# Second-layer outer weight sums formed in DRAM by accumulating transfers during the recurrent stage

## The reference

```
merged = (jax.nn.sigmoid(gate_a) * (att @ p['w_branch_a'])
          + jax.nn.sigmoid(gate_b) * (rwkv_y @ p['w_branch_b']))
x = x + merged @ p['w_out']
hm = _rmsnorm(x, p['norm_mlp'])
x = x + jnp.square(jax.nn.relu(hm @ p['w_mlp_in'])) @ p['w_mlp_out']
```

## Time and profile before

| what | value |
|---|---|
| median of three runs | 2492.46 us |
| the three runs | 2480.7, 2492.46 and 2493.25 us |
| the profiled execution's own time | 2478.53 us |
| span in that profile, first to last instruction | 2476.8 us |
| PE busy over the span | 92% |
| DVE busy | 65% |
| ACT busy | 33% |
| POOL busy | 18% |
| mean granted PE clock, share of full | 0.969 |

### The profile page before, as it was taken

How to read it: one execution, slowest core, us unless ns; L and a number is a source line. 1 busy time by engine, 2 the same in 40 slices (tenths; PEclk the granted TensorE clock), 3 DMA queues, 4 the chain that set the end, 5 groups by cost and what they waited for, 6 DMA issues and landing times. The chain is left out here.

```text
span 2476.8 us, 48938 instructions
## 1 busy us (share of the span) xinstructions
PE 2284.6 (92%) x19275; PEld 1701.0 (69%) x19275; DVE 1603.3 (65%) x3005; ACT 806.6 (33%) x1425; POOL 434.4 (18%) x354
## 2 busy tenths in 40 slices
PE   6999999999899999898899889999999999989986
PEld 4566788765656566665665668787778778878865
DVE  3257888965556565345557556648975775776687
ACT  4235888424334342224455532111121111111101
POOL 0020000000000000001101102025354354344340
PEclk8989999999999999898999999999999999999998
DMA  6441232343232313247877744505226326315402
GB/s 188 121 119 63 64 104 71 122 151 102 57 102 59 97 47 105 76 109 225 284 244 258 235 177 148 170 21 200 81 65 191 102 65 184 109 56 178 124 1 81
DMA packets 270656, 306.78 MB, mean 124 GB/s; under 512 B 56230, under 2 KB 183047, under 8 KB 270300
## 3 DMA queue, kind: packets, MB, share of 16 engines
q1 hardware_dynamic: 195316, 252.78, 32.3%
q10 hardware_dynamic: 75112, 50.87, 7.3%
HBM read 239.78 MB, written 62.23 MB: 122 GB/s over the span
## 5 line engine op out<-in xcount | busy, mean ns | idle before, releaser
L1286 PE MATMUL rwkv_banks<-gate_sides_then_att_T 128*128 128x384 f32 (+1 forms) x768 | 280.4, 498 | 7.8 <-PEq L441 3.7
L1286 PEld LDWEIGHTS rwkv_banks<-gate_sides_then_att_T 128*128 128x128 f32 x768 | 139.4, 197 | 76.5 <-issue 19.4
L3606 DVE TENSOR_TENSOR merged_then_hidden<-merged_then_hidden,ps_mm 128x544 f32<-128x544 f32 x180 | 127.8, 715 | 81.9 <-PE ps_mm L3331 78.1
L3331 PE MATMUL ps_mm<-gate_sides_then_att_T,w_mm 128*128 128x272 f32 x584 | 147.6, 400 | 7.8 <-ACT merged_then_hidden L3399 5.4
L600 PE MATMUL first_banks<-hT,w_pr 128*128 128x384 f32 (+3 forms) x432 | 144.3, 491 | 4.6 <-PEq L188 4.6
L3331 PEld LDWEIGHTS ps_mm<-gate_sides_then_att_T,w_mm 128*128 128x128 f32 x584 | 113.0, 194 | 33.3 <-ACT merged_then_hidden L3399 5.8
L910 DVE TENSOR_SCALAR_CACHE_REDUCE _and_tildes_then_k_pages<-scores,mid 128x384 f32<-128x384 f32 (+4 forms) x150 | 131.5, 876 | 3.1
L600 PEld LDWEIGHTS first_banks<-hT,w_pr 128*128 128x128 f32 (+1 forms) x432 | 81.0, 192 | 62.2 <-issue 21.3
L3413 ACT ACTIVATE merged_then_hidden<-merged_then_hidden 128x1088 f32<-128x1088 f32 x32 | 35.6, 1111 | 260.6 <-DVE merged_then_hidden L3618 260.6
L3331 PE MATMUL ps_mm<-right_blocks,w_mm 128*128 128x272 f32 x408 | 101.8, 394 | 3.3 <-DVE sums_of_right_sides_ L3606 3.3
L2376 POOL MEMSET gate_sides_then_att_T<- 128x136 f32 x1 | 0.2, 212 | 596.3 <-POOLq L1181 596.3
(11 more groups left out here) (619 smaller groups left out, 5227.1 us busy)
## 6 DMA issues: line engine op xcount, KB each, us to landing
v_pages<-in_cache_v SPq DMA_DIRECT2D x128, 256.0 KB, 5.3
gate_sides_then_att_T<-in_w_in ACTq DMA_DIRECT2D x46, 512.0 KB, 4.3
_and_tildes_then_k_pages<-in_cache_k SPq DMA_DIRECT2D x88, 256.0 KB, 3.4
gate_sides_then_att_T<-right_blocks_d SPq DMA_DIRECT2D x82, 272.0 KB, 2.7
right_blocks<-right_blocks_d SPq DMA_DIRECT2D x65, 272.0 KB, 2.7
T_and_gates_then_weights<-in_w_mlp_in SPq DMA_DIRECT2D x16, 1024.0 KB, 5.2
T_and_gates_then_weights<-in_w_mlp_out SPq DMA_DIRECT2D x16, 1024.0 KB, 5.5
w_pr<-in_w_in SPq DMA_DIRECT2D x27, 512.0 KB, 5.2
```

Source lines behind the costliest of these rows:

```text
L1286: ins = MM(B[:, gate_bank(n), 0:w], gw[:, n % 2, k_, :], hc[:, k_, 0:w], start=(k_ == 0), stop=(k_ == KO - 1))
L3331: ins = nc.tensor.matmul(ps[:, bank, 0:272], w, right[:, k, :], start=(k == 0 and step in f.OPENS), stop=(k == 1), skip_group_check=True)
L3606: V.tensor_tensor(to, of, f.pair(ps, q, step), ALU.add).then_inc(f.by_dve, 1)
```

## The change

The outer sums of second layers are no longer made by DVE. A new method, called by POOL's program of the recurrent stage after its memsets, makes them in a DRAM tensor `sums_d` (4 sums x 4 groups x 1 MB), each as a copy and an accumulating transfer, and POOL waits for each transfer before it issues the next. That is 8 transfers a group and 32 in all. The accumulation can only add, so S2, S3 and S4 are formed with the opposite sign of a11 or a12, and the signs of the spreading of results follow (DVE's `spread_results`, same number and size of operations). In the MLP stage SP loads, for each second layer, seven pieces of 1 MB (a11, a12, a22 and the four sums) in place of four. `weight_sums` runs for first layers alone. In second layers S2 lies in the buffer s4 and S4 in the buffer s2 (`left_2`), so that each of the seven is loaded when the quarter that stands at the same place in the layer before has finished.

```diff
+    def add_in_dram(self, pool, w_2, r, which):
+        to = dict(zip(("s1", "s2", "s3", "s4"), self.sums_d[:, r]))
+        w = w_2.rearrange("(r k c) (m e) -> k m r c e", k=2, c=512, m=2)
+        a11, a12, a21, a22 = w[0, 0, r], w[1, 0, r], w[0, 1, r], w[1, 1, r]
+        for name, (u, v) in (("s1", (a21, a22)), ("s3", (a21, a11)), ("s2", (to["s1"], a11)), ("s4", (to["s2"], a12))):
+            if name in which:
+                for of, op in ((u, None), (v, ALU.add)):
+                    if op:
+                        self.nc.gpsimd.dma_start(to[name], of, accum_op=ALU.add).then_inc(self.w_sums, 16)
+                    else:
+                        self.nc.gpsimd.dma_start(to[name], of).then_inc(self.w_sums, 16)
+                    self.sums_made += 16
+                    pool.wait_ge(self.w_sums, self.sums_made)
...
             p.clear_last(pool)
-
+            for r in range(FF // D):
+                p.add_in_dram(pool, a["w_mlp_out"], r, ("s1", "s3", "s2", "s4"))
...
+    held = {**quarter, "s1": s1, "s2": s2, "s4": s4}
+    summed_before = ("s1", "s4", "a21", "s2")
+    left_2 = {**left, "P6": s4, "P3": s2}
...
-        if name in ("P1", "P4", "P2"):
-            n = {"P1": "a11", "P4": "a22", "P2": "a12"}[name]
-            if layer % 2:
-                eng.wait_ge(q_in[n], 16 * layer + 16)
-            else:
-                eng.wait_ge(q_scaled[n], 2 * layer + 4)
+        if layer % 2:
+            n = {"P1": "a11", "P4": "a22", "P2": "a12", "P5": "s1", "P6": "s4", "P7": "a21", "P3": "s2"}[name]
+            eng.wait_ge(q_in[n], 16 * (layer + 1 if n in quarter else (layer + 1) // 2))
+        elif name in ("P1", "P4", "P2"):
+            eng.wait_ge(q_scaled[{"P1": "a11", "P4": "a22", "P2": "a12"}[name]], 2 * layer + 4)
         else:
-            eng.wait_ge(l_summed, 4 * layer + {"P5": 1, "P6": 2, "P7": 3, "P3": 4}[name])
+            eng.wait_ge(l_summed, 2 * layer + {"P5": 1, "P6": 2, "P7": 3, "P3": 4}[name])
...
+                users = [{"a11": "P1", "a12": "P2", "a21": "P7", "s1": "P5", "a22": "P4", **more}
+                         for more in ({"s2": "P6", "s4": "P3"}, {"s4": "P6", "s2": "P3"})]
                 for n in range(2 * R):
-                    for name, user, sums in (("a11", "P1", 3), ("a12", "P2", 4), ("a21", "P7", 3), ("a22", "P4", 1)):
+                    r = n // 2
+                    order = layers[n - 1] if n else UP
+                    user = users[(n + 1) % 2]
+                    for name in sorted(held if n % 2 else quarter, key=lambda name: order.index(user[name])):
...
-                        if n % 2:
+                        if n % 2 and name in summed_before:
+                            src = p.sums_d[summed_before.index(name), r]
+                        elif n % 2:
...
-                for n in range(2 * R):
+                for n in range(0, 2 * R, 2):
```

More of the change, by code:

```diff
@@ L3100, in merge_and_mlp @@
     gate_in = [p.sem(f"mm_gate_in{n}") for n in range(2)]
-    q_in, q_scaled = ({n: p.sem(f"ml_{what}_{n}") for n in quarter} for what in ("in", "scaled"))
+    q_in = {n: p.sem("ml_in_" + n) for n in held}
+    q_scaled = {n: p.sem("ml_scaled_" + n) for n in quarter}
     moved = [p.sem(f"ml_moved{n}") for n in range(f.RING)]
@@ L3224, in inner_sums @@
             def inner_sums(q):
-                base, to = left[names[q]], inner[q % 2]
+                base, to = (left, left_2)[q // 7 % 2][names[q]], inner[q % 2]
                 def free(step):
@@ L3278, in product @@
             def product(q, step):
-                name, base, e = names[q], left[names[q]], inner[q % 2]
+                name, base, e = names[q], (left, left_2)[q // 7 % 2][names[q]], inner[q % 2]
                 r, first_layer = q // 14, q % 14 < 7
@@ L3561, in weight_sums @@
                     if n:
-                        dve.wait_ge(*f.product(nth[n - 1]["P6"], "P4"))
+                        dve.wait_ge(*f.product(nth[n - 1]["P3"], "P4"))
                     else:
                         dve.wait_ge(d.made, 14 * ML)
-                    dve.wait_ge(l_summed, 4 * n + 1)
+                    dve.wait_ge(l_summed, 2 * n + 1)
                     V.tensor_tensor(s2, s1, a11, ALU.subtract).then_inc(l_summed, 1)
@@ L3646, in spread_results @@
                 last = nth[2 * R - 1]
-                for after, step, pairs in (("P1", "P4", ((x11, y1),)), ("P5", "P4", ((x12, y5), (x22, y5))),
-                                           ("P6", "P4", ((y6, y1), (x12, y6))),
-                                           ("P7", "P4", ((y7, y6),)), ("P4", "P3", ((x21, y7), (x22, y7)))):
-                    for n, (to, of) in enumerate(pairs):
+                for after, step, sums in (("P1", "P4", ((x11, x11, y1, ALU.add),)),
+                                          ("P5", "P4", ((x12, x12, y5, ALU.subtract), (x22, x22, y5, ALU.add))),
+                                          ("P6", "P4", ((y6, y6, y1, ALU.subtract), (x12, x12, y6, ALU.subtract))),
+                                          ("P7", "P4", ((y7, y6, y7, ALU.subtract),)),
+                                          ("P4", "P3", ((x21, x21, y7, ALU.add), (x22, x22, y7, ALU.add)))):
+                    for n, (to, u, v, op) in enumerate(sums):
                         for m, rows in enumerate((up, down)):
@@ L3654, in spread_results @@
                                 dve.wait_ge(*f.kept(last[after], step))
-                            ch.done(V.tensor_tensor(to[:, rows, :], to[:, rows, :], of[:, rows, :], ALU.add))
+                            ch.done(V.tensor_tensor(to[:, rows, :], u[:, rows, :], v[:, rows, :], op))
             weave(merge_out(), x_sums(), right_blocks(), weight_sums(), rstds(), gather(), finish(), hidden_sums(),
```

23 lines of the change are left out of this document (12 added, 11 removed).

## The result

The changed kernel takes 2500.26 us in the median against 2489.93 us for the kernel before, measured side by side: ratio 1.0050, 95% interval 1.0033 to 1.0067 (a ratio here and below is not the quotient of the two medians, which is 1.0041 in this case). The forecast was 2467 us, with a range that ended at 2494. The profiled execution has a span of 2498.7 us and took 2500.46 us in all.

What follows compares the result with a forecast made beforehand. PE was taken to bound the MLP and recurrent stages, with small holes. 26.8 us won less 6 and 2 paid gave 18.8, so 2478.5 became 2460 us, plus 7 for the median: 2467 us, range 2450 to 2494.

Steps and rivals of the forecast that it cites:

- The recurrent stage, opening: Recurrent stage's first units: gate weight loads land late beside POOL's transfers and PE waits; 6 us taken, 0 to 7.1.
- The recurrent stage, the rest: Recurrent stage after its opening: DVE's operations may be held by POOL; 2 us taken, bounds 0 and 17.
- The chain of POOL: Recurrent stage: POOL's 32 transfers one after another take 427 us, 170 to 613, ending some 160 us before the stage.
- The overrun: First rival, recurrent stage: transfers over 18.5 us each make all engines wait for POOL; 2574 us at 22 each; chance 0.13.
- The MLP part: MLP second layers: PE's holes beside DVE's outer sums go, 26.8 us won in layers 1, 3, 5 and 7; 12 at least.
- the hidden sums of 2.49 us stay where they were: MLP second layers: DVE's hidden sums remain unchanged, and banks are free in time with little to spare.
- The extra loads at nothing: MLP stage: twelve more 1 MB loads on SP's queue cost nothing; without cover each late block costs up to 5.3 us.
- The recurrent stage pays all along: Second rival: each transfer holds a DVE operation 1.0 us, 17 us reach the path, 2477 us, no change; chance 0.16.
- the 8 in the sum: Recurrent stage's cost in the forecast: 6 us for the opening and 2 us for the rest.
- Holes stay: Third rival, MLP: DVE stays late by hidden sums and spreading, only POOL's wait goes; 2475 us; chance 0.13 with the fourth.
- signs of being wrong: POOL last at the recurrent stage's end; gate loads landing in 7 us or more; idle over 2 us before hidden sums.
- The median: Whole kernel: median after put 7 us above the profiled execution's 2460 us, half way between; 2467 us.

Runs made afterwards that it cites:

- e10: The changed kernel with the recurrent stage's 46 gate weight loads cut to one eighth of their rows: 2483.09 us, ratio 0.9984 to the kernel before.
- e12: The changed kernel with gate weight loads cut to one eighth and the gates' stores issued from SyncE's queue: 2482.05 us, ratio 0.9965 to the kernel before.
- e9: The changed kernel with its 32 transfers spread over the recurrent stage behind its opening, one about every 17 us: 2496.23 us, ratio 1.0040 to the kernel before.
- e8: The changed kernel with transfers moved to the projection stage and two POOL waits for hidden sums per second layer: 2462.84 us, ratio 0.9907 to the kernel before.
- e5: The kernel before, unchanged, run once more for a second trace of its recurrent stage: 2491.27 us, one run.

## Why the prediction was wrong, step by step

**The recurrent stage, opening: right in kind, somewhat short.** I took 6 us (0 to 7.1) for late gate weight loads. At before's 585.9 us, behind the opening, the changed kernel's trace was 9.6 us late, and the five others with its loads and transfers in that place were 6.8 to 10.8; the kernels without transfers were 0.0 to 1.3. The waits are those that I named, and with small loads the lateness was gone (e10, e12).

**The recurrent stage, the rest: the step that failed.** "2 us for the rest of the stage", bounds 0 and 17. By the times it is 25 us less the opening's 7 to 10, so 15 to 18 us, and by the traces more. I had measured slack for the loads ("several us to spare") and stopped there. What I put at next to nothing without a row are two consumers of the same engines that have no slack at all: a store whose issuing instruction stands on the engine that computes, and TensorE's instructions. By experiment the first is worth some 7 us, give or take 6; the second, with the lower clock behind its pauses, is argued from traces at about 10 of idle time and as much again of slower products. The first could have been read before: in the kernel before the store at 695.34 us took 1.85 us, beside two loads of 768 KB, where the median is 0.51. And my bound of 17 came from a mechanism, DVE held by POOL, that does not happen here: VectorE's operations kept their lengths. It was near to the size by chance.

**The chain of POOL: right in kind, too long.** 427 us taken, 277 measured, below the middle of 170 to 613. An adding transfer takes 9 to 10 us where I took 16.0, a copy between sums 5.7 where I took 10.7. A copy takes hardly longer than a load alone, 5.3 us, so reading and writing overlap. The overrun did not come. Nor did the rule of the Trainium skill show that I had weighed (SBUF — State Buffer, section "Who interferes with whom"), by which a fast one-source operation and POOL's descriptor writing lock each other out: VectorE's durations are unchanged, and POOL's issuing instructions took 0.5 to 1.3 us.

That the transfers were quicker is no comfort, though. They put the same bytes into less time, and in e9 twice the time made no difference that could be measured.

**The MLP part: right in kind, 26.8 us taken, 11 to 15 measured by the times and 16.8 in the trace.** By layers: 3.0 forecast and 3.1 in the trace, 7.0 and 2.4, 9.6 and 6.7, 7.2 and 5.5; layer 0 lost 1.0. The holes beside the outer sums went (2.43 us in layer 7 became 0.38). In layer 3 the hole in front of P3 was 2.40 us and not the 4.09 that I had read in layer 7 and taken for all three. What failed is the sentence "the hidden sums of 2.49 us stay where they were": they stayed, and became 4.09 and 3.55 us, since POOL's sums now run at the same time. Three holes of 2.52 us, 7.6 us, are most of the 10 that are missing in the trace; without POOL beside them they are 1.3 us each (e8), so not all of it is POOL's. The earlier trace rows had the sign: the second pair of hidden sums, beside POOL, took 4.10 us there, and I wrote that down as a hole of another kind.

**The extra loads at nothing: right.** The loads of second layers land in 5.2 to 5.6 us in the median, 5.5 before, and first layers stay at 89.84.

**The rivals.** "The recurrent stage pays all along" (0.16) is what happened, by other mechanisms. Its 17 us on top of the 8 in the sum make 25, the size that was measured, and that is luck. "Holes stay" happened in part. Together they give the sign: the sum for the profiled kind of execution was -26.8 + 8, and is -15 + 25. Of the signs of being wrong only the last came, idle times over 2 us beside the hidden sums. POOL was not the last at the end of the stage, and the gate weight loads landed in 5.7 us in the median, not in 7.

**The median.** I added 7 us since the median lay above the profiled execution. A good part of the reason is in the table: that execution had an unusually short recurrent stage, 8.4 us under that of e5, which took 12.7 us longer in all.

## What to carry to other kernels

Idle transfer engines are not free room in a stage of many short steps: ask who needs those engines with no slack, and count the stores that a computing engine issues and TensorE's instruction stream among them. The same 32 MB cost 25 us among some 4200 short products and nothing measurable among 1200 long ones, and neither spreading them nor dropping the adding helped measurably; moving them did. And when a change frees an engine from a wait, look at what it will run beside: the freed engine's work can slow its neighbour's.

## What the runs showed of the hardware that I had not expected

- TensorE's instructions arrive as 16 KB transfers over the shared engines, about one for 250 of them. In this stage that is one each 8 us, and with the transfer engines busy at 0.84 the pauses next to them grow from 10 to 12 us to 19 to 25.
- An instruction that issues a transfer can hold its engine: 7.18 us on ScalarE, with the work behind it in order. With loads of 64 KB in front of it in place of 512 KB the longest was 1.20 us (e10). The Trainium skill (DMA: Bandwidth & Descriptors, section "Queues, rings and completion order") says that each transfer engine goes around the queues that have work, a packet at a time. With that the small transfers should not wait for whole megabytes, and the trace agrees: the median gate weight load landed in 5.7 us in place of 4.4, while a transfer beside it took 9.6.
- A 1 MB copy from DRAM to DRAM takes 5.7 us (long rows) to 7 us, an added one 9 to 10 (8.7 to 12.6), all of it with POOL's issue.
- The same code takes 597 to 612 us in the recurrent stage from one execution to the next, with TensorE idle for 52 to 55 us each time: the difference goes with the granted clock, 0.97 to 0.94. A single trace can be 10 us off in one stage, so differences between traces have to be held against the times.
